# Two transformer blocks on one core: where the scan's B and C loads, the head turns and two gate products stand, and a gather ring of nine buffers for eight

## The reference

```python
def first_block(x, ...):
    h = rms_norm(x, mix_norm_g)
    q, k, v, u, gate_a, gate_b = split(h @ w_in)          # 2048, 512, 512, 1024, 2048, 2048
    y_a = windowed_gqa(norm(q), norm(k), v, attn_sink) @ w_attn_o    # 16 heads on 4 of k, v
    y_ssm = s5(u, dir 0, forward) + s5(u, dir 1, backward) + ssm_d * u
    y_act = gelu(y_ssm)
    y_b = (y_act @ glu_w_a) * sigmoid(y_act @ glu_w_b)
    x = x + (sigmoid(gate_a) * y_a + sigmoid(gate_b) * y_b) @ w_out
    return x + peer(rms_norm(x), w_query, keys, expert_down, expert_up)

def s5(u, ...):     # 64 groups of 16 channels, 64 complex states each, per direction
    lam_bar = exp(lam * step);  bu = u @ (((lam_bar - 1) / lam) * B)
    states = scan(a * s + b);   return real(states @ C)

def windowed_gqa(q, k, v, sink):   # |distance| <= 128, slopes, a sink in the softmax
    s = q @ k.T * scale - slopes * dist;  m = max(max(s), sink);  p = exp(s - m)
    return (p / (sum(p) + exp(sink - m))) @ v

def peer(h, ...):   # 8 heads, 128 x 128 = 16384 experts, the best 16 of each head
    idx, gate = top 16 of (top 16 of q1 @ keys1) x (top 16 of q2 @ keys2)
    w = gate * gelu(einsum('tkd,td->tk', expert_down[idx], h))
    return einsum('tk,tkd->td', w, expert_up[idx])
```

## Time and profile before

| | before |
|---|---|
| median of 3 runs | 3790.36 us (3787.3 to 3792.3) |
| the profiled execution | 3787.29 us, its span 3785.6 us |
| PE busy | 3355.3 us (89%) |
| DVE busy | 2594.5 us (69%) |
| ACT busy | 740.9 us (20%) |
| POOL busy | 1241.2 us (33%) |
| mean granted TensorE clock | 0.919 of full |
| DMA | 1075.65 MB, mean 284 GB/s |
| of it the gathers (queue q0) | 728.77 MB, 49.5% of the engines' time |
| scan | 76 to 571 us |
| attention of the first block | 575 to 754 us |
| expert stages | 1000 to 2196 and 2616 to 3786 us |

### The profile page before, as it was taken

How to read it: one execution, slowest core, us unless ns; L and a number is a source line. 1 busy time by engine, 2 the same in 40 slices (tenths; PEclk the granted TensorE clock), 3 DMA queues, 4 the chain that set the end, 5 groups by cost and what they waited for, 6 DMA issues and landing times.

```text
span 3785.6 us, 41300 instructions
## 1 busy us (share of the span) xinstructions
PE 3355.3 (89%) x13892; PEld 1803.2 (48%) x13892; DVE 2594.5 (69%) x5312; ACT 740.9 (20%) x1731; POOL 1241.2 (33%) x1133
## 2 busy tenths in 40 slices
PE   8999998899998888778888899999998877788887
PEld 7443444444875554443222258458755544432222
DVE  3887885565588889996555431525888889975554
ACT  1222224400110114651000002211101136510000
POOL 0000000000244455565444400002454555665454
PEclk9999999999999998667999999999999986689999
DMA  6443432244689999999999963425999998999999
GB/s 210 133 131 116 131 127 91 100 157 161 268 341 389 401 404 371 341 373 376 360 393 380 390 223 119 156 89 221 360 397 386 391 342 320 363 381 380 370 381 345
DMA packets 316861, 1075.65 MB, mean 284 GB/s; under 512 B 94332, under 2 KB 103436, under 8 KB 214668
## 3 DMA queue, kind: packets, MB, share of 16 engines
q0 software_dynamic: 147456, 728.77, 49.5%
q1 hardware_dynamic: 115808, 301.49, 22.3%
q10 hardware_dynamic: 53392, 42.83, 3.5%
HBM read 1415.93 MB, written 2.10 MB: 375 GB/s over the span
## 4 chain that ended last, share of the span: by engine, by line
PE 43%; DMA 27%; DVE 18%; issue 7%; POOL 2%; ACT 1%; ACTq 1%; DVEq 0%; POOLq 0%; another core or an unknown queue 0%; SPq 0%
DMA big<-in_peer_down,sc 10%; DMA big<-in_peer_u,sc 10%; PE bank L747 9%; DVE sc L2437 5%; PE bank L761 4%; PE bank L1204 4%; DVE sc L2440 4%; PE bank L1138 4%; PE bank L1124 4%; PE bank L997 3%; DMA big<-in_peer_up,sc 2%; PE bank L921 2%; DMA big<-in_peer_v,sc 2%; PE bank L986 2%; POOL big L681 2%
## 5 line engine op out<-in xcount | busy, mean ns | idle before, releaser
L2437 DVE CUSTOM_DVE_ANT_0 sc<-big,hs 128x1024 f32<-128x1024 f32 x480 | 587.8, 1225 | 457.3 <-DMA big<-in_peer_down,sc 237.0
L1124 PE MATMUL bank<-big,sc 128*32 128x512 f32 x4096 | 634.7, 709 | 156.4 <-DMA big<-in_peer_up,sc 82.9
L2440 DVE CUSTOM_DVE_ANT_0 sc<-big,hs,sc 128x1024 f32<-128x1024 f32 x480 | 616.7, 1285 | 17.1
L1204 PE MATMUL bank<-wring 128*128 128x512 f32 x1024 | 515.3, 639 | 69.9 <-DMA wring<-in_dense_up 51.9
L1188 PE MATMUL bank<-ht,wring 128*128 128x256 f32 x2048 | 511.6, 402 | 1.4 <-ACT wring L1650 0.9
L1188 PEld LDWEIGHTS bank<-ht,wring 128*128 128x128 f32 x2048 | 393.6, 199 | 195.0 <-issue 138.1
L747 PE MATMUL bank<-wring,ht 128*128 128x512 f32 x1024 | 457.6, 602 | 0.0
L681 POOL DMA_INDIRECT big<-in_peer_down,sc x256 | 300.4, 1174 | 337.0 <-DVE sc L2440 210.9
L681 POOL DMA_INDIRECT big<-in_peer_u,sc x256 | 303.7, 1186 | 325.5 <-DVE sc L2440 188.3
L681 POOL DMA_INDIRECT big<-in_peer_up,sc x256 | 300.3, 1173 | 269.1 <-PE bank L1124 146.1
L681 POOL DMA_INDIRECT big<-in_peer_v,sc x256 | 306.8, 1198 | 246.0 <-PE bank L1124 142.8
(11 more groups left out here) (431 smaller groups left out, 3667.3 us busy)
## 6 DMA issues: line engine op xcount, KB each, us to landing
wring<-in_w_in SPq DMA_DIRECT2D x84, 1024.0 KB, 5.6
wring<-in_dense_down SPq DMA_DIRECT2D x64, 1024.0 KB, 9.0
wring<-in_w_out SPq DMA_DIRECT2D x32, 1024.0 KB, 5.1
wring<-in_dense_up SPq DMA_DIRECT2D x128, 256.0 KB, 7.2
wring<-in_dense_up ACTq DMA_DIRECT2D x128, 256.0 KB, 7.5
wring<-in_w_attn_o SPq DMA_DIRECT2D x16, 1024.0 KB, 5.0
wring<-in_peer_w_query SPq DMA_DIRECT2D x16, 1024.0 KB, 9.0
wring<-in_peer_w_q SPq DMA_DIRECT2D x16, 1024.0 KB, 5.2
```

What stands on the lines that cost most here:

```text
L1124: mm = pe.matmul(acc_bank[j][32 * q:32 * q + 32, :], w_blocks[:, u % 2, g, :], gslot[:, m % RING, q * 512:(q + 1) * 512], start=(u % PH == ...
L1204: mm = pe.matmul(dense_out[t][:, :], dense_w[:, r, t * P:(t + 1) * P], sup[:, i % UP_RING, :], start=(r == 0), stop=(r == DENSE - 1))
L2437: st.link(v.tensor_tensor_reduce(dot_out[:, 0:cut_at], row[:, 0:cut_at], h[:, u // PH, 0:cut_at], 1.0, start, ALU.mult, ALU.add, acc))
L2440: v.tensor_tensor_reduce(dot_out[:, cut_at:D], row[:, cut_at:D], h[:, u // PH, cut_at:D], 1.0, start, ALU.mult, ALU.add, acc).then_inc(dot ...
```

## The change

It has three parts, and a setting that goes with the third.

1. *Scan.* `reload_bc(k)` is called inside ScalarE's `ssm_tile`, in step s == 1 behind the raw phases of step 2 (and behind a bank copy if one is due there), and no longer behind the tile.
2. *Attention.* TensorE turns a head behind six parts of `glu_w_a` and no longer behind eight; part seven stands before the first two scores, part eight behind them. VectorE's two gate products stand in units 3 and 4, one each, and no longer both in unit 4.
3. *Gathers.* `RING` is 9. Since 512 is no multiple of 9, the buffer and the semaphore's count of a gather go on over both stages (`ring_slot`, `landed`). `big` grows by 8 KB a partition; `dynamic_dma_scratch_size` is set to 8192 bytes, where no size was given before.

```diff
-RING = 8
+RING = 9
...
+def ring_slot(layer, m):
+    return (layer * GATHERS + m) % RING
+
+def landed(layer, m):
+    return 16 * ((layer * GATHERS + m) // RING + 1)
...
-        big = sb("big", SLOTS * SLOT)
+        big = sb("big", RING * SLOT)
...
             def slot_free(layer, m):
-                if m == 6:
+                if m < RING and ring_slot(layer, m) == 6:
                     pool.wait_ge(keys_evac, 4 * (layer + 1))
                 m -= RING
...
-                    out=gslot[:, m % RING, :], out_offset=None, in_=table[0],
+                    out=gslot[:, ring_slot(layer, m), :], out_offset=None, in_=table[0],
...
             def attention_head(j, b0, r, used):
-                for b in (b0, b0 + 1):
-                    for kk in range(KS):
-                        glu_part(b, r, used, kk)
+                for i in range(2 * KS - 2):
+                    glu_part(b0 + i // KS, r, used, i % KS)
                 for t in range(NT):
                     pe.wait_ge(qk_ready, j + 1)
...
+                glu_part(b0 + 1, r, used, KS - 2)
                 pe.wait_ge(qk_tevac, j * 3 + 3)
                 scores(0)
                 scores(1)
+                glu_part(b0 + 1, r, used, KS - 1)
                 for u in range(UA):
...
-                pe.wait_ge(row_full[m % RING], 16 * (layer * (GATHERS // RING) + m // RING + 1))
+                pe.wait_ge(row_full[ring_slot(layer, m)], landed(layer, m))
...
+                    if s == 1 and k + 1 < SSM_K:
+                        reload_bc(k)
...
             for k in range(SSM_K):
                 ssm_tile(k)
-                if k < SSM_K - 1:
-                    reload_bc(k)
...
-                    if u == 4:
+                    if u in (3, 4):
                         v.wait_ge(wused[4 * g + 1], r + 1)
-                        for t_ in range(NT):
-                            v.tensor_tensor(gb(t_), dense_bank[t_][:, :], gb(t_), ALU.mult).then_inc(pair_evac[0], 1)
+                        v.tensor_tensor(gb(u - 3), dense_bank[u - 3][:, :], gb(u - 3),
+                                        ALU.mult).then_inc(pair_evac[0], 1)
...
-    nc = _bacc.Bacc("TRN2", target_bir_lowering=False, num_devices=1)
+    nc = _bacc.Bacc("TRN2", target_bir_lowering=False, num_devices=1,
+                    dynamic_dma_scratch_size=8192)
```

More of the change, by code:

```diff
@@ L197, in two_blocks @@
         wslot = wring[:, :].rearrange("p (s c) -> p s c", s=SLOTS)
-        gslot = big[:, :].rearrange("p (s c) -> p s c", s=SLOTS)
+        gslot = big[:, :].rearrange("p (s c) -> p s c", s=RING)
         x = xs[:, :].rearrange("p (t c) -> p t c", t=NT)
@@ L681, in fetch @@
                 pool.indirect_dma_start(
-                    out=gslot[:, m % RING, :], out_offset=None, in_=table[0],
+                    out=gslot[:, ring_slot(layer, m), :], out_offset=None, in_=table[0],
                     in_offset=bass.IndirectOffsetOnAxis(ap=index, axis=0),
-                    bounds_check=NKEY * NKEY - 1, oob_is_err=False).then_inc(row_full[m % RING], 16)
+                    bounds_check=NKEY * NKEY - 1, oob_is_err=False).then_inc(row_full[ring_slot(layer, m)], 16)
             def popularity_constants(layer):
@@ L1121, in row_sums @@
                     pe.wait_ge(acc_used, 32 * layer + 4 * (j + 1))
-                pe.wait_ge(row_full[m % RING], 16 * (layer * (GATHERS // RING) + m // RING + 1))
+                pe.wait_ge(row_full[ring_slot(layer, m)], landed(layer, m))
                 for q in range(4):
                     mm = pe.matmul(acc_bank[j][32 * q:32 * q + 32, :], w_blocks[:, u % 2, g, :],
-                                   gslot[:, m % RING, q * 512:(q + 1) * 512], start=(u % PH == 0 and g % 4 == 0),
+                                   gslot[:, ring_slot(layer, m), q * 512:(q + 1) * 512], start=(u % PH == 0 and g % 4 == 0),
                                    stop=(u % PH == PH - 1 and g % 4 == 3), skip_group_check=True)
@@ L2432, in row_dot @@
                     v.wait_ge(dots_done, n)
-                v.wait_ge(row_full[m % RING], 16 * (layer * (GATHERS // RING) + m // RING + 1))
-                row, acc = gslot[:, m % RING, :], sub(rAC)[:, u % 2 * TOPK + k:u % 2 * TOPK + k + 1]
+                v.wait_ge(row_full[ring_slot(layer, m)], landed(layer, m))
+                row, acc = gslot[:, ring_slot(layer, m), :], sub(rAC)[:, u % 2 * TOPK + k:u % 2 * TOPK + k + 1]
                 start, cut_at = 0.0, D // 2 if u else 0
```

## The result

The changed kernel takes 3740.04 us (median of 4 runs, 3738.84 to 3745.22) where the kernel before, beside it, takes 3791.33: a ratio of 0.9864, 95% interval 0.985 to 0.9877. It is 51 us faster (47 to 57). The forecast was 3754 us, the range 3736 to 3772. The direction and two of three terms held; the term for the ninth buffer was too small.

The account below looks back on a forecast made before the run. TensorE's own work was taken to bound the scan, TensorE's waits to cost time in attention, and nearly full DMA engines to limit the expert stages. -16.6 - 8.2 + 0 - 9.2 = -34.0 us gave 3754 us, range 3736 to 3772.

Parts of the forecast that it names:

- the term for the ninth buffer: Expert stages: one more gather under way fills some DMA idle time, -9.2 us, bounds 0 and -25.
- The scan, 17.3 us for 16.6: Scan tiles: earlier loads of B and C remove TensorE's idle time and a slow clock, -16.6 us, bounds -11 and -18.
- The chain: Scan, tile's end: late loads delay GpSimd's padding, TensorE waits 0.81 us, 8.44 in the late tile, then runs at 1.2 GHz.
- The rival in which the padding blocks VectorE: Scan: VectorE stands still during the 3.0 us padding, seven times, +17 us, 3771 us in all; chance 0.03.
- Attention, 9.6 us for 8.2: Four heads: turns behind six parts bring the first softmax 2.3 us earlier, 1.3 in head 1; -8.2 us, bounds 0 and -8.9.
- The gate products, 0 for 0: Attention, fourth and fifth units: without time to spare in any unit, each product costs half the wait, 2 x 0.6; 0 us.
- the bound of -4.8: Attention, gate products: best case 4 x 1.2 us won, if VectorE idles there for want of scores.
- I count two spells a stage: Expert stages: ring full at the start and at the end of VectorE's stretch, 2.3 us each, -9.2 in both stages.
- only queues here: Expert stages, where DMA engines are busy 0.98 or 0.99: a ninth gather only queues, landing after some 15 us for 12.6.
- The store: Descriptor store: nine gathers hold 81 of 512 places; rival, GpSimd runs out of room, 3864 us, chance 0.04.
- ring gives much: Expert stages, rival: landings stay at 12.6 us and a third of the idle time returns, -25, 3737.5 us; chance 0.08.
- the rival of the late sine: Scan: eight loads take twice 6.2 us, VectorE 4.8 us late seven times, +34, 3796 us; chance 0.04, half in full.

Follow-up runs that it names:

- behind the fourth sine: Changed kernel with the loads of B and C issued behind ScalarE's fourth sine instead of the second; one execution, 3732.34 us, only its trace read.
- -0.1 and -0.1 alone: Kernel before with nine gather buffers and the descriptor store of 8192 bytes, nothing else; 3765.55 us, ratio 0.9921.
- scan alone: Kernel before with only the loads of B and C moved behind the second sine; 3772.61 us for 3793.41, ratio 0.9947.

## Why the prediction was right, and where it was not

*What bounds.* Read by stages, the profile gave the right limits for the scan and attention, and each part moved its own stage only. That the expert stages are full, so that the idle hundredths are not to be had, was wrong (the ninth buffer, below).

*The scan, 17.3 us for 16.6.* The tiles are 58.75 us for the forecast 58.7. The chain was right in all its links: the padding's wait (L645), the late tile's 8.44 us, the slow clock behind it. Three sizes were off without harm.

The eight issues took 4.7 us and not 6.2, and began 1.5 us sooner than forecast, under the raw phases, so the sine was not late by 1.8 but by nothing. The weight transfer was issued beside them, as forecast, but 1.95 us behind the first of the eight, where it was 0.06 us behind in rows 4. Over the traces of before and after, eight issues take 4.17 us where SyncE's comes 2.9 us behind the first or later, 4.3 to 5.2 where it comes 1.95 us behind it, and 6.2 to 6.5 where it comes with it. TensorE's new wait for VectorE's last sum is 0.35 us a tile for 0.2. Against that its busy time a tile fell to 58.4 us, where the sum had kept 58.6; that fits the overlap described under attention.

The rival in which the padding blocks VectorE is tested by one run. In the changed kernel the padding missed VectorE's work in six tiles of seven (1.48 us, most of it in the 1.75 us wait); behind the fourth sine it met some of that work and cost nothing. No run puts all four products beside VectorE's products with both inputs in SBUF in mid-tile, as they stood at the tile's end before.

The Trainium skill, SBUF — State Buffer, section Who interferes with whom, has the two engines take the port pair in turn, each for a whole instruction. By that rule VectorE should have lost about as long as the padding's four products last. The rows at the tile's end before show less: in the 3.0 us of padding from 197.38 VectorE's instructions lost 0.6 us in all, at most 0.20 each (L2033, 0.88 for 0.68), and the padding's products took up to 0.84 us for 0.40. Behind the fourth sine VectorE lost 0.0 to 0.7 us a tile.

*Attention, 9.6 us for 8.2.* Mis-sized by 0.3 to 0.4 us a head. The prediction came to 2.3 us, little more than the idle times, 0.88 and 1.34, as it laid the groups end to end. A stop cost more. In the records of a row without a stop the next group starts 0.16 us before the last one's end (612.88 + 0.38 = 613.26, next 613.10), and that overlap is lost at each. 0.88 + 1.34 + 2 x 0.16 = 2.54, near the measured 2.63 up to the first turn of probabilities. The six parts ended at 10.30 us of the head, where 10.47 were taken.

*The gate products, 0 for 0.* Right, and for the reason given, but "no unit has time to spare" holds only for the place ahead of the division. Right behind it every unit had 0.96 us or more, and the product moved there wins the 1.2 us a head that the bound of -4.8 had named.

*The ninth buffer, 26 us over all traces for 9.2 (19.3 in the profiled pair, 28 by medians alone).* This is the term that was mis-sized, and the step that failed is: "I count two spells a stage". The start, one of the two, gave nothing (-0.3 and -0.5 us in the pair, -0.1 and -0.1 alone, and some 120 us with seven buffers too). The VectorE stretch gave 1.0 and 2.2 in the pair, 1.8 and 4.0 over all traces, where 2.3 each were forecast; whether by the mechanism named no run tells. The two stretches set at nothing, because the engines were busy 0.99 and 0.98, gave 17 of the 19, and 20 of the 26. The share was read as "only queues here", although the idle hundredths had been counted a few lines above as 12.9 us of each stage's 37. The runs with 7, 8 and 9 buffers show the rate of these stretches following the ring's length. What exactly is idle in them (which of the 16 engines, at what moment of a gather) no run here tells. One candidate that was not tested is the skipped rows: if they fall unevenly on the 16 engines, a longer queue evens them out. The bound, a third of all idle time or -25, was near the truth: 26 is a third of the 75. By the rival's words, though, a third comes back if the landings stay at 12.6 us; it came back although they rose to 15.0. The prediction had also written that it is wrong if the expert stages shorten by over 25 us; by the mean of the traces they do, just.

*The store.* At nothing, as forecast; the run with the store alone shows it. The 147456 packets of the 1024 gathers are 144 each, nine for each of 16 engines, as the prediction took them.

*The sum.* -34.0 forecast, -48.2 in the trace: +0.7 from the scan, +1.4 from attention, +10.1 from the ring, and 2.0 that belong to no part (the clock in the second block, the first 82 us). With the mean of the traces the ring's error is 16.8. All three errors have the same sign, so none hid another; the time lies inside the range because the ring's bound of -25 had gone into it, which is what the ring came to. The rival "ring gives much" (-25 for the ring) came nearer than the forecast and had a chance of 0.08, too small. One sum of the prediction is incomplete: the rival of the late sine, +34 - 16.6 - 8.2, leaves out the ring's -9.2; with it the time is 3787 and not 3796.

## What to carry to other kernels

A DMA share of 0.98 is not 1: in the last stretch here, 459 us long, its idle hundredths came to 9 us, and a ninth buffer took 6 of them; going from seven to eight had given more. A gain of this size is read from several traces of each kernel, not from one pair. Before a moved instruction is set at nothing or at half, look at both sides of the instruction that is waited for: the idle time stood right behind the division and not ahead of it. A removed stop of TensorE was worth its idle time and the overlap of two neighbouring groups, here 0.16 us more.

## What the runs showed of the hardware

- GpSimd's four products of 128x128 take 1.48 us where VectorE waits, 1.5 to 2.7 where it works behind the fourth sine, and took up to 3.12 at the tile's end, beside VectorE's products of 128x512 with both inputs in SBUF, 0.68 us that became 0.88. Behind the fourth sine a scan of 128x256 went from 0.68 to 0.88 us too. Beside products that read one input from a bank both engines kept their times (0.40 us a padding product, 0.68 to 0.69 for L2021 and L2022). What runs beside them decides by how much both stretch.
- A load issued by ScalarE's queue costs 0.4 to 0.5 us of its time, up to 1.5 where SyncE issues a weight transfer beside it (eight took 4.17 to 6.5 us). The activations ahead of it still ran while the first ones were being issued (L1524 at 149.08 between loads at 148.12 and 149.63).
- Single runs of one kernel differ by 10 us and more (before: 3786.8 to 3802.14 in one set). In the traces it is the expert stages that differ most (2351 to 2361 us with eight buffers). The work ahead of them, up to the first gathers, repeats within 5 us: it ends at 988.14 to 992.95 in the five traces in which it is that of the kernel before but for at most the gate products. Part of this is the clock: the start of the first head takes 22.5 us at a granted clock of 0.93 (before) and 23.7 at 0.88 (scan alone).
